# Cached key and value pages moved to other steps of a hybrid decoder layer

## The chip, the core and the metric

The kernel runs on one core of a Trainium2 chip. The metric is device time in microseconds of one execution; lower is better. The core's engines are TensorE (PE; PEld is its weight load), VectorE (DVE), ScalarE (ACT), GpSimd (POOL) and SyncE (SP); each runs its own instruction stream in order, and they wait for each other through semaphores. SyncE, ScalarE and GpSimd also issue DMAs, each into a queue of its own.

## The reference

One layer of a decoder for 512 new prompt rows and for eight sequences that add one row each to a past of 4096 rows. Cut to what matters:

```python
xn = rms_norm(x, norm1_g)
proj = xn @ w_in                                     # 2048 -> 5128 columns
u_pool, h_b, h_c, h_x, q, k, v, f_logit = split(proj)
y_pool = causal_pool_mix(u_pool, ...)                # window means, 4 groups
y_conv = h_b * causal_dwconv(h_c * h_x, ...)         # 3 taps
y_att = attn_fn(rms_norm(q), rms_norm(k), v, log_sigmoid(f_logit + b_f))
x = x + concat(rms_norm(y_pool), rms_norm(y_conv), rms_norm(y_att)) @ w_o
a, gate = split(rms_norm(x) @ w_up)
x = x + (silu(causal_dwconv(a, ...) + b) * gate) @ w_down
```

For the prompt, `attn_fn` is causal attention with 8 heads of 128 over the 512 rows themselves. For the eight sequences it is

```python
k_past = cache_k[l, page_table].reshape(db, past, N_HEADS, HEAD_DIM)
v_past = cache_v[l, page_table].reshape(db, past, N_HEADS, HEAD_DIM)
s = q . k - (decay of the forget gates);  p = softmax(s);  o = p @ v
```

with pages of 128 rows: 32 pages a sequence, 256 in all. A page of keys and a page of values is 512 KB each, so the caches are 268 MB of what the kernel reads.

## The kernel before

Prompt rows and sample rows stand side by side as 520 columns. Weights are loaded 2 MB at a time (`load_raw`, by SyncE), split into a head and a rest by ScalarE and VectorE (`head`, `weight_rest`), and multiplied on TensorE in three passes (`products`, `out_chunk`).

All engines walk through the same **steps** `s`, numbered 0 to 174, and at each step issue what belongs to it:

- steps 0 to 79: the input projection, a chunk of weights each;
- steps 82 to 93 (`MIX0` = 81, `HEAD0` = 93): the pooling and convolution mixers. `pool_part` runs on VectorE in steps 81, 84, 87 and 90, and TensorE's `pool_mix` one step later;
- steps 93 to 141: the eight prompt heads, one each six steps (`HSTEP`), seven stages each. Stage 1 is the sum of squares on TensorE, stage 4 the row maximum on VectorE, stage 5 the transposes, stage 6 the product with the values;
- step 142 (`TAIL`): the end of the mixers' norm; here SyncE also reloads the residual;
- steps 143 to 174 (`OUT0` on): the output projection, 32 chunks of 24 matmuls (`out_chunk`).

The cached pages are woven into these steps. `page_slots` fixes which page belongs to which step; from its tables `KEYS` and `VALUES` every engine takes its part:

- a **key page** is loaded by SyncE (`page`, line 584) into one of four buffers (`kring`), as soon as VectorE has used the page that was in it; VectorE's `key_page` (line 1802) multiplies it with the query and sums, head by head. In a step VectorE takes the first key page ahead of `pool_part` and `conv_part`, the second at the end of the step;
- a **value page** is loaded by GpSimd (`value_loads`, line 505) into one of four buffers (`vring`) as soon as TensorE has used the page in it; TensorE's `value_page` multiplies it with the probabilities. In the steps of the projection the first two pages stand within the chunk (after its third or fifth block) and the others behind it; in the steps of the heads, the first two of four stand ahead of the head's own matmuls, otherwise all stand behind them;
- `value_places` assigns the buffers. A value page whose step lies between the end of all keys (`K_END[-1]`) and `TAIL` goes round eight buffers, the four of the keys included; those in key buffers are loaded by SyncE (line 645), and the first of each waits until all 256 key pages are used. Before, no step fulfils the condition;
- when the last key page of a sequence has been used, a softmax over its 4096 scores runs in small pieces over the next eight steps (`softmax`, `misc`), and its values can begin six steps later; when its values end, sixteen small matmuls (`t_quad` in the rows) bring its output into columns one step later.

Before, a step has two key pages, and none from 82 to 93; the keys end at step 141. Value pages of the heads' steps come two at a time in two steps of three, and in all steps from 82 to 93 and from 142 on in the pattern 4, 4, 2; they end at step 169. Two lines of SyncE's loop load the first weights of the output projection in steps 107 and 111, beside the heads; six further loads of 2 MB follow in the projection (line 570), each after `sample_out`, a small product that stands behind every fourth chunk (the rows with `t_wraw` on TensorE).

Of the kernel before, what the change touches and what calls it, by code (L numbers as in the profile page):

```python
# [28 lines left out]
PAGES = PAST // P  # L29
# [20 lines left out]
CHUNKS = 80  # L50
MIX0 = CHUNKS + 1
HEAD0 = MIX0 + 12
STAGES = 7
HSTEP = 6
TAIL = HEAD0 + (HEADS - 1) * HSTEP + STAGES
KEY0 = 2
K_RATE = 2


def page_slots():  # L60
    keys, values, k_end, v_end = {}, {}, [], []
    slots = [s for s in range(KEY0, TAIL) if not MIX0 < s <= HEAD0]
    for n in range(DEC * PAGES):
        keys.setdefault(slots[n // K_RATE], []).append(n)
    for r in range(DEC):
        k_end.append(slots[(PAGES * (r + 1) - 1) // K_RATE])
    at = 0
    for r in range(DEC):
        at = max(at, k_end[r] + 6)
        done = 0  # L70
        while done < PAGES:
            rate = ((2 if at % 2 == 0 else 0) if at < CHUNKS else (2 if at % 3 else 0) if HEAD0 < at < k_end[-1] else
                    (4 if at % 3 else 2))
            take = min(rate, PAGES - done)
            if take:
                values[at] = [r * PAGES + done + i for i in range(take)]
            done += take
            at += 1
        v_end.append(at - 1)
    return keys, values, k_end, v_end  # L80


KEYS, VALUES, K_END, V_END = page_slots()
EARLY = TAIL - STAGES
OUT0 = TAIL + 1
# [2123 lines left out]
```

How the kernel before makes its waits and increments, by code:

```python
        def step(eng, count, ins):  # L340
            count.inc(ins)
            eng.wait_ge(count.sem, count.value())
# [81 lines left out]
        def copy_piece(eng, copy, q, n, j, done):  # L425
            eng.wait_ge(z_full, n + 1)
            bank = ps[:, 4 + n % 4, :]
            if j < 4:
                copy(orow[:, q, j, :], bank).then_inc(done, 1)
            else:
                copy(srow[:, q * 512:(q + 1) * 512], bank[0:DEC]).then_inc(done, 1)
# [4 lines left out]
        @block.gpsimd  # L436
        def _(pool):
            cst = Count(const_ready)
            cst.inc(pool.memset(ident[:, :], 0.0))
            cst.inc(pool.memset(ones[:, :], 1.0))
            cst.inc(pool.memset(cmask[:, :], 0.0))
            cst.inc(pool.memset(tri[:, :], 1.0))
            for t in range(16):
                cst.inc(pool.memset(rc[:, t:t + 1], 1.0 / (t + 1)))
            cst.inc(pool.memset(epsc[:, :], EPS))
            pool.wait_ge(const_ready, cst.value())
            cst.inc(pool.affine_select(out=ident[:, :], in_=ident[:, :], compare_op=ALU.not_equal, fill=1.0,
                                       base=0, pattern=[[-1, P]], channel_multiplier=1))
# [3 lines left out]
            cst.inc(pool.affine_select(out=tri[:, :], in_=tri[:, :], compare_op=ALU.is_ge, fill=0.0,  # L453
                                       base=0, pattern=[[-1, P]], channel_multiplier=1))
            pool.wait_ge(const_ready, cst.value())
            tv = tri.rearrange("p (a c) -> p a c", c=PAGES)
# [59 lines left out]
            pool.wait_ge(z_act, 3)
            for b in range(DEC):
```

## Time and profile before

| | us |
|---|---|
| median of 3 runs | 2842.98 |
| lowest and highest | 2842.80, 2843.91 |
| the profiled execution | 2841.29 |
| its span, first to last instruction | 2839.4 |
| TensorE busy | 2651.8 (93%) |
| VectorE busy | 1426.1 (50%) |
| ScalarE busy | 732.9 (26%) |
| DMA, mean rate over the span | 188 GB/s |

The mean shares hide the stages: the feed-forward from about 1300 us on is nearly all TensorE, and the traffic of the caches lies before it. So the table of the whole says little on this change; the rows further down are cut by stage. A busy share there is that of one stretch.

### The profile page before, as it was taken

Reading aid. Unit: us, or ns where it says so; the run is one execution under the profiler, and the core shown is the slowest. Engines: PE = TensorE matmul, PEld = TensorE weight load, DVE = VectorE, ACT = ScalarE, POOL = GpSimd, SP = SyncE. Lnnn points to the kernel's source line nnn. Section 1 sums busy time; section 2 is a strip of 40 time slices with the busy share of each in tenths; the row PEclk is TensorE's granted clock in tenths of the full one; section 3 lists DMA queues with packets and bytes.
Section 4 is the critical chain, followed back from the end, with each engine's and each line's share of the span. In section 5 each row is a group of like instructions: output and inputs, shape, how many; then the busy total and the mean of one; then the engine's idle time right before and its main releaser. Section 6 shows DMA issues by size and latency. Waiting matters only on the chain.

```text
span 2839.4 us, 50530 instructions
## 1 busy us (share of the span) xinstructions
PE 2651.8 (93%) x19656; PEld 2325.7 (82%) x19656; DVE 1426.1 (50%) x5629; ACT 732.9 (26%) x981; POOL 156.6 (6%) x317
## 2 busy tenths in 40 slices
PE   5899999977768699989999999999999999999998
PEld 3799989952333255659999999999999999999998
DVE  4787776765778732234434343434343434343433
ACT  4332212212333521133222222222222222222221
POOL 0100000012101122200000000000000000000000
PEclk7999999988867699989999999999999999999999
DMA  7689999998999887753222222222223222222221
GB/s 242 239 285 328 332 344 341 338 363 283 376 358 355 289 294 262 271 186 130 91 90 90 90 90 90 90 90 90 93 101 100 95 90 90 90 90 90 90 90 64
DMA packets 274531, 532.93 MB, mean 188 GB/s; under 512 B 16410, under 2 KB 177787, under 8 KB 272980
## 3 DMA queue, kind: packets, MB, share of 16 engines
q1 hardware_dynamic: 214573, 361.52, 37.1%
q0 software_dynamic: 39472, 142.46, 13.7%
q10 hardware_dynamic: 20247, 25.73, 2.5%
q8 instruction: 154, 2.52, 0.4%
q14 instruction: 85, 0.70, 0.1%
HBM read 503.94 MB, written 24.05 MB: 186 GB/s over the span
## 4 chain that ended last, share of the span: by engine, by line
PE 79%; DMA 7%; DVE 7%; issue 2%; ACT 2%; SPq 1%; ACTq 0%; POOL 0%; POOLq 0%; DVEq 0%
PE ps L711 78%; DVE t_work L1802 4%; DMA t_r<-in_cache_k 4%; DMA t_r<-in_cache_v 2%; DMA t_wraw<-in_w_in 1%; PE ps L714 1%; DVE t_xl L1639 0%; DVE t_stg L1695 0%; DVE t_nmax L1940 0%; SPq L584 0%; DVE t_wl L1639 0%; DVE t_work L1639 0%; DVE t_auxL L1947 0%; SPq L570 0%; ACT L1425 0%
## 5 line engine op out<-in xcount | busy, mean ns | idle before, releaser
L711 PE MATMUL ps<-t_xh,t_wh 128*128 128x260 f32 (+1 forms) x4352 | 949.1, 293 | 11.9 <-DVE t_xl L1639 11.8
L711 PE MATMUL ps<-t_xh,t_wl 128*128 128x260 f32 (+1 forms) x4352 | 935.7, 291 | 0.0
L711 PE MATMUL ps<-t_xl,t_wh 128*128 128x260 f32 (+1 forms) x4352 | 934.1, 290 | 0.0
L1639 DVE TENSOR_TENSOR t_wl<-t_wraw,t_wh 128x1024 fp32r<-128x1024 f32 x376 | 459.9, 1224 | 870.2 <-ACT t_wh L1236 870.2
L1236 ACT ACTIVATE t_wh<-t_wraw 128x1024 fp32r<-128x1024 f32 x376 | 398.1, 1060 | 1644.0 <-PE ps L711 1643.8
L711 PEld LDWEIGHTS ps<-t_xh,t_wh 128*128 128x128 f32 x4352 | 685.5, 190 | 94.2 <-issue 63.8
L711 PEld LDWEIGHTS ps<-t_xh,t_wl 128*128 128x128 f32 x4352 | 685.8, 189 | 11.8
L711 PEld LDWEIGHTS ps<-t_xl,t_wh 128*128 128x128 f32 x4352 | 685.4, 189 | 9.1
L1802 DVE CUSTOM_DVE_ANT_0 t_work<-t_r,t_work 128x128 f32<-128x128 f32 x2048 | 454.5, 285 | 154.9 <-DMA t_r<-in_cache_k 142.7
L711 PE MATMUL ps<-t_hh,t_wh 128*128 128x260 f32 x1408 | 285.8, 284 | 3.4 <-issue 3.4
L711 PE MATMUL ps<-t_hh,t_wl 128*128 128x260 f32 x1408 | 284.7, 284 | 0.0
L711 PE MATMUL ps<-t_hl,t_wh 128*128 128x260 f32 x1408 | 283.0, 282 | 0.0
L711 PE MATMUL ps<-t_r,t_work 128*8 128x512 f32 x1040 | 186.9, 670 | 67.2 <-DMA t_r<-in_cache_v 52.2
L1639 DVE TENSOR_TENSOR t_r<-ps,t_r 128x520 f32<-128x520 f32 (+1 forms) x184 | 128.5, 698 | 228.2 <-PE ps L711 228.2
L711 PEld LDWEIGHTS ps<-t_hh,t_wh 128*128 128x128 f32 x1408 | 218.3, 189 | 4.2 <-issue 3.7
L711 PEld LDWEIGHTS ps<-t_hl,t_wh 128*128 128x128 f32 x1408 | 217.3, 189 | 0.0
L711 PEld LDWEIGHTS ps<-t_hh,t_wl 128*128 128x128 f32 x1408 | 216.8, 189 | 0.0
L505 POOL DMA_DIRECT2D t_r<-in_cache_v x256 | 136.1, 532 | 959.2 <-PE ps L711 915.2
L1802 DVE DVE_READ_ACCUMULATOR2_ANT t_S<- 128x1 f32 x2048 | 164.6, 80 | 0.1
L711 PEld LDWEIGHTS ps<-t_r,t_work 128*8 128x8 f32 x1040 | 19.4, 88 | 148.7 <-DMA t_r<-in_cache_v 98.7
L520 POOL DMA_DIRECT2D out_ffn_sample<-t_aux x8 | 4.1, 518 | 1554.6 <-ACT t_aux L1236 1554.6
L1643 DVE SCALAR_TENSOR_TENSOR t_work<-t_work 128x8 f32<-128x8 f32 (+1 forms) x176 | 78.2, 486 | 3.1
(256 smaller groups left out, 1197.0 us busy)
## 6 DMA issues: line engine op xcount, KB each, us to landing
t_r<-in_cache_k SPq DMA_DIRECT2D x256, 512.0 KB, 7.2
t_r<-in_cache_v POOLq DMA_DIRECT2D x256, 512.0 KB, 6.5
t_wraw<-in_w_up SPq DMA_DIRECT2D x44, 2048.0 KB, 8.0
t_wraw<-in_w_in SPq DMA_DIRECT2D x22, 2048.0 KB, 11.6
t_wraw<-in_w_down SPq DMA_DIRECT2D x22, 2048.0 KB, 7.8
t_wraw<-in_w_o SPq DMA_DIRECT2D x11, 2048.0 KB, 12.2
scr_proj<-t_stg ACTq DMA_DIRECT2D x40, 256.0 KB, 5.5
t_aux<-scr_proj ACTq DMA_DIRECT2D x8, 768.0 KB, 18.4
```

The costliest lines, as they stand in the source:

```text
L505: pool.dma_start(vring[:, b, :], v_pages[bass.ds(g, 1), :, :].rearrange("a p n -> (a p) n")).then_inc(v_loaded[b], 16)
L520: pool.dma_start(o["ffn_sample"][0, b, 1, :].rearrange("(t n) -> t n", n=P), astrows[:, b, :]).then_inc(states_copied, 16)
L711: return pe.matmul(out, lhsT, rhs, start=start, stop=stop)
L714: return pe.transpose(out, in_, ident[0:n, 0:n])
L1236: return act.activation(out, in_, ACT.Copy)
L1639: return dve.tensor_tensor(out, in0, in1, op)
L1643: return dve.scalar_tensor_tensor(out, in0, scalar, in1, ALU.mult, ALU.add)
L1802: last = dve.tensor_tensor_reduce(out=junk[:, h * HD:(h + 1) * HD], in0=kring[:, p % RING, h * HD:(h + 1) * HD], in1=qcur[r % 2][:, h * HD ...
```

## The change

`page_slots` alone is changed. Its new table of slots gives a step one key page in steps 82 to 93 and two elsewhere (`K_RATE`), where there were none and two. With twelve more pages placed there, the keys end at step 135 instead of 141. Value pages keep their rule up to step 79 and, in fact, their places up to step 93; in the heads' steps while keys run they come two at a time in every odd step; from step 136 to 141 in the pattern 4, 4, 2, in eight buffers; from step 142 on four in every step, so that they end at step 165 instead of 169. In numbers: steps 94 to 135 hold 42 value pages (56 before), steps 136 to 141 hold 20 (10 before), step 142 holds 4 in both, and the projection 92 (88 before).

```diff
-    slots = [s for s in range(KEY0, TAIL) if not MIX0 < s <= HEAD0]
+    slots = [s for s in range(KEY0, TAIL) for _ in range(1 if MIX0 < s <= HEAD0 else K_RATE)]
     for n in range(DEC * PAGES):
-        keys.setdefault(slots[n // K_RATE], []).append(n)
+        keys.setdefault(slots[n], []).append(n)
     for r in range(DEC):
-        k_end.append(slots[(PAGES * (r + 1) - 1) // K_RATE])
+        k_end.append(slots[PAGES * (r + 1) - 1])
...
-            rate = ((2 if at % 2 == 0 else 0) if at < CHUNKS else (2 if at % 3 else 0) if HEAD0 < at < k_end[-1] else
-                    (4 if at % 3 else 2))
+            rate = ((2 if at % 2 == 0 else 0) if at < CHUNKS else (2 if at % 2 else 0) if HEAD0 < at < k_end[-1] else
+                    2 if at % 3 == 0 and at < TAIL else 4)
```

On TensorE, around steps 135 to 137, the order before was this (a row with `t_r,t_work` is a value page's product, two rows a page; `t_aux,t_ones 128x512 x2` are the sums of the last head's stage 1, `t_work,t_ones 128x512` is the total of a mixer's norm):

```order
L711 MATMUL ps<-t_auxL,t_aux 128x128
L714 MATMUL ps<-t_ident,t_aux 128x128 x4
L711 MATMUL ps<-t_work,t_ones 128x512
L711 MATMUL ps<-t_aux,t_ones 128x512 x2
L711 MATMUL ps<-t_r,t_work 8x512 x4
L711 MATMUL ps<-t_aux,t_ones 128x128
```

and it is this after the change:

```order
L711 MATMUL ps<-t_auxL,t_aux 128x128
L714 MATMUL ps<-t_ident,t_aux 128x128 x4
L711 MATMUL ps<-t_work,t_ones 128x512
L711 MATMUL ps<-t_r,t_work 8x512 x8
L711 MATMUL ps<-t_aux,t_ones 128x512 x2
L711 MATMUL ps<-t_r,t_work 8x512 x8
L711 MATMUL ps<-t_aux,t_ones 128x128
```

Four pages (138 to 141, eight rows) now stand ahead of the head's stage 1, the last two of them in key buffers.

On TensorE, at the seam between the heads and the projection, the piece before was this (`t_auxL,t_aux` are the last head's products with the values, `t_xh,t_wh` the projection's first matmul):

```order
L711 MATMUL ps<-t_quad,t_work 128x1 x8
L711 MATMUL ps<-t_auxL,t_aux 128x512
L711 MATMUL ps<-t_auxL,t_aux 128x384
L711 MATMUL ps<-t_auxL,t_aux 128x256
L711 MATMUL ps<-t_auxL,t_aux 128x128
L711 MATMUL ps<-t_r,t_work 8x512 x8
L711 MATMUL ps<-t_work,t_ones 128x512
L711 MATMUL ps<-t_r,t_work 8x512 x4
L711 MATMUL ps<-t_xh,t_wh 128x512
```

and it is this after the change:

```order
L711 MATMUL ps<-t_auxL,t_aux 128x512
L711 MATMUL ps<-t_auxL,t_aux 128x384
L711 MATMUL ps<-t_auxL,t_aux 128x256
L711 MATMUL ps<-t_auxL,t_aux 128x128
L711 MATMUL ps<-t_r,t_work 8x512 x8
L711 MATMUL ps<-t_work,t_ones 128x512
L711 MATMUL ps<-t_r,t_work 8x512 x4
L711 MATMUL ps<-t_ps,t_ones 128x8
L711 MATMUL ps<-t_quad,t_work 128x1 x8
L711 MATMUL ps<-t_xh,t_wh 128x512
```

The small matmuls of the sequence whose values end (`t_quad`), and a sum of the last softmax (`t_ps`), moved from ahead of the head's last stage to right ahead of the projection.

## Rows read from the trace of the kernel before

**Rows 1.** The page, 40 equal slices of 71 us, busy tenths.

```profile
PE   5899999977768699989999999999999999999998
DMA  7689999998999887753222222222223222222221
```

**Rows 2.** Windows by stage: length, then busy us (instructions) by engine, clock, DMA share, GB/s.

```profile
606.90:650.00 43.10, 26.85 (x110) 9.43 (x103) 21.46 (x84) 9.18 (x15) 8.07 (x16) 0.63 0.84 311
650.00:697.10 47.10, 33.04 (x144) 8.01 (x144) 21.75 (x53) 10.55 (x19) 17.39 (x33) 0.96 0.89 302
697.10:938.30 241.20, 180.83 (x631) 82.47 (x631) 190.19 (x1451) 82.66 (x155) 29.83 (x56) 0.75 0.98 364
759.00:806.00 47.00, 26.72 (x92) 11.86 (x91) 29.16 (x222) 14.04 (x26) 4.23 (x8) 0.71 1.03 389
938.30:981.00 42.70, 28.25 (x110) 14.00 (x112) 36.95 (x225) 23.33 (x38) 4.24 (x8) 0.68 0.69 231
1003.50:1239.20 235.70, 227.39 (x1196) 139.84 (x1194) 59.01 (x81) 43.05 (x58) 44.53 (x85) 0.99 0.74 257
```

**Rows 3.** Waits of TensorE in the mixers, 606.9 to 697.1: us, times, longest.

```profile
PE ps L711 <- DMA t_r<-in_cache_v: 25.1, 22, 5.4
PE ps L711 <- DVE t_auxW L1889: 1.9, 1, 1.9
```

**Rows 4.** Waits of VectorE, 697.1 to 938.3; the last row, 755 to 808.

```profile
DVE t_work L1802 <- DMA t_r<-in_cache_k: 32.4, 20, 7.0
DVE t_work L1639 <- ACT t_stg L1404: 5.1, 3, 4.2
DVE t_aux L1934 <- ACT t_aux L1429: 3.3, 1, 3.3
DVE t_denall L1827 <- PE ps L711: 2.5, 1, 2.5
...
DVE t_work L1802 <- DMA t_r<-in_cache_k: 21.4, 8, 7.0
```

**Rows 5.** The page, costliest groups: all key pages on VectorE, eight instructions a page.

```profile
L1802 DVE CUSTOM_DVE_ANT_0 t_work<-t_r,t_work 128x128 f32<-128x128 f32 x2048 | 454.5, 285 | 154.9 <-DMA t_r<-in_cache_k 142.7
```

**Rows 6.** Projection: TensorE's waits, then its timeline at a late and a timely pair.

```profile
PE ps L711 <- DMA t_r<-in_cache_v: 2.4, 3, 1.2
...
1050.77 0.40 PE L711 MATMUL ps<-t_xh,t_wl 128*128 128x512 f32 x1
1051.73 1.03 PE L711 MATMUL ps<-t_r,t_work 128*8 128x512 f32 x4 [0.56 <-DMA t_r<-in_cache_v]
...
1054.93 0.50 PE L711 MATMUL ps<-t_xh,t_wh 128*128 128x512 f32 x1
...
1199.15 0.40 PE L711 MATMUL ps<-t_xh,t_wl 128*128 128x512 f32 x1
...
1200.45 0.50 PE L711 MATMUL ps<-t_xh,t_wh 128*128 128x512 f32 x1
```

**Rows 7.** Timeline: end of VectorE's last key instruction of step 135, then TensorE to the projection.

```profile
937.80 0.08 DVE L1802 DVE_READ_ACCUMULATOR2_ANT t_S<- 128x1 f32 x1
...
937.88 1.99 PE L711 MATMUL ps<-t_aux,t_ones 128*128 128x512 f32 x4 [0.33 <-ACT t_aux L1421]
...
967.06 1.90 PE L711 MATMUL ps<-t_r,t_work 128*8 128x512 f32 x8 [9.04 <-issue]
...
972.59 3.41 PE L711 MATMUL ps<-t_quad,t_work 128*128 128x1 f32 x16
...
989.33 1.88 PE L711 MATMUL ps<-t_r,t_work 128*8 128x512 f32 x4 [2.71 <-DMA t_r<-in_cache_v]
```

**Rows 8.** SyncE's weight loads from 1010; issues at 1039 to 1041 and 1044 to 1046, landing us.

```profile
1010.38 171.02 SPq L570 DMA_DIRECT2D t_wraw<-in_w_o  x6
...
t_r<-in_cache_v POOLq DMA_DIRECT2D x2, 512.0 KB, 4.4
...
t_r<-in_cache_v POOLq DMA_DIRECT2D x2, 512.0 KB, 7.9
```

## Prediction

> **What bounds the kernel now.** I read the page's 40 slices first, to find the place: TensorE is at 9 tenths in nearly every slice, but at 6 to 9 tenths in slices 8 to 13, while the DMA row stands at 8 or 9 until slice 16 and at 2 to 3 after that [rows 1]. The change lies wholly in slices 8 to 17; the feed-forward behind them isn't touched. Then I cut that part by stage [rows 2]: the mixers (steps 82 to 93, 90.2 us in two halves), the heads while keys still run (steps 94 to 135, 241.2 us), the last head (steps 136 to 141, 42.7 us), the seam before the output projection, and the projection (235.7 us). Each has a limit of its own.
>
> - **Mixers**: no engine is full. TensorE waits 25.1 us for value pages [rows 3]. The four value buffers are reloaded as fast as pages land; the DMA share is 0.84 and 0.89 [rows 2].
> - **Heads with keys**: DMA share 0.98 at 364 GB/s, and VectorE busy 190.2 of 241.2 us [rows 2]. So both are near full. VectorE waits 32.4 us for key pages, of which 21.4 us fall into the 53 us in which two weight loads of the output projection pass [rows 4].
> - **Last head**: DMA is idle for a third of the time (0.69) and VectorE is busy for 37.0 of 42.7 us [rows 2].
> - **Projection**: TensorE is busy 227.4 of 235.7 us [rows 2], with DMA waits of 2.4 us in all [rows 6]. Here a page costs what its matmuls cost.
>
> **The change, part by part.** The sum is made against the profiled run, 2841.3 us with its span of 2839.4 us; it lies 1.7 us below the median of 2842.98.
>
> *Mixers, twelve key pages more: +10 us.* A page is 512 KB. While DMA was full, 47.0 us at 389 GB/s [rows 2], a page took 0.524 MB / 389 GB/s = 1.35 us, so twelve are 16.2 us of DMA time. Before, four keys (pages 160 to 163) were loaded ahead here and left lying; now each used key frees a buffer and starts another load. Two or so of those loads fall into the first half, where 16% of 43.1 us is idle and hides them. Ten fall into the second: 13.5 us, and idle there is 11% of 47.1 us, 5.2 us. The remaining 8.3 us lengthen the landings of the value pages, on which TensorE already waits. On VectorE a key page is 454.5 us / 256 = 1.8 us [rows 5]; VectorE is idle for more than half of the stretch, so eleven of the twelve are hidden, but the one in step 84 stands ahead of the second pooling part, for which TensorE waited 1.9 us [rows 3]: +1.9. Bounds: 0, if DMA takes all twelve in its gaps, and 16.2 + 1.9 = 18.1, if none. I take 10, since the nearest row, the second half, says that the gaps there are small.
>
> By the Trainium skill ("DMA: Bandwidth & Descriptors", Specifications), a core draws about 358 GB/s from its memory at most. By that the mixers have (358 - 306) GB/s x 90.2 us = 4.7 MB to spare for 6.3 MB, and the rest would take 4.4 us, so this term would be 6 and not 10 (306 being the mean of the two halves). The trace moved 389 GB/s for 47 us [rows 2], so that is no ceiling here, and the measurement decides.
>
> *Heads with keys, 42 value pages for 56: -15 us.* Values come every second step instead of two steps in three: 14 pages fewer, and at the end no four keys are loaded ahead: 18 x 1.35 = 24.3 us of DMA time out of 241. Two keys a step stay, so VectorE's work stays. The gain is in its waits. Outside the weight loads these are 32.4 - 21.4 = 11.0 us in short pieces, and a tenth less traffic should leave 2: -9. Beside the weight loads three pages are gone: 3 x 1.35 = -4. TensorE has two pages fewer for each head, mostly hidden: -2. Then VectorE is next: 190.2 us busy, some 12 us in the small gaps between instructions, and about 11 us of waits for ScalarE and TensorE [rows 4] make 213, so more than -28 can't be. Bounds: -8 and -28.
>
> *Last head and seam: +4 us.* All keys are used at the end of step 135, and six steps hold 20 value pages instead of 10. Eight buffers serve them, four being the keys' own; but pages 140 to 143 come first, in exactly those four, and TensorE must use 140 and 141 at the head of step 136, ahead of the head's own matmuls. Before, VectorE ended the keys of step 135 at 937.9 us, and TensorE began the sums of the last head at 937.88 [rows 7]. Now the first load can be issued only then; a pair lands in a median of 4.4 us when DMA is light [rows 8], at 942.6 and 943.8 or so with the issue. TensorE brings 2 us of its own (two pages are new in step 135), waits some 3 us, and uses two more pages: the sums start near 944.4, +6.5 us. Behind that, ten more pages are 8 to 10 us of TensorE (0.95 us each: two pages are eight matmuls in 1.90 us), but TensorE stood idle for 9.04 us before 967.06 [rows 7], and they go there. Keys no longer delay VectorE; still ScalarE's normalizations stand in the same chain, so I give 2.5 us back, no more. In the seam TensorE waited 2.71 us before 989.33 for a page that was late [rows 7]; that wait goes, and the sixteen small matmuls of an ended sequence, which before stood in step 140 (at 972.59, 3.41 us [rows 7]), now stand right ahead of the projection: 0. Bounds: -5 (the idle 9 us vanish and the first loads land early), +9 (nothing is given back).
>
> *Projection, four pages in every step: +14 us.* 46 pairs of pages instead of 44 stand in it. A pair holds up the projection's matmuls by 1.3 us (1199.15 to 1200.45 [rows 6]): +2.6. The larger part is late pages. Each four steps SyncE issues a 2 MB weight load, six in this stretch [rows 8], right before the second pair of a step is used and reloaded. The loads issued next to it took 7.9 us, against 4.4 us without [rows 8]. With four pages in two successive steps the same buffers are due one step later, and that is too soon: from 1050.77 to 1054.93 is 4.2 us instead of 1.3, 2.9 us lost [rows 6]. Before, the pattern 4-4-2 met this fully once in six, the other times a step with two pages or other work lay between. Now all six meet it: 6 x 2.9 = 17.2, less about 5 us paid before, less a little for what the stall itself lets land: +11. Bounds: +2.6 (the loads land in time) and +15.
>
> Sum: 10 - 15 + 4 + 14 = +13, so 2854 us for a profiled run and 2855.5 us for the median.
>
> **The rivals.**
> - *DMA time is only moved (faster).* Keys hide in the mixers' gaps, and the page landings nowhere grow. For it: 12 us of DMA time are idle there; VectorE's waits show that the heads want it. The price: mixers +2, heads -20, last head +4, projection +2.6: -11, 2832 us. It decides if value pages in the mixers still land about as fast with keys beside them. Against it: TensorE already waits on just these landings.
> - *Key waits vanish almost entirely (no change).* Heads -26 instead of -15, the rest as forecast: +2, 2845 us. For it: 24.3 us of DMA time freed. Against: two thirds of the waits belong to two 2 MB loads, which stay.
> - *The last head pays in full (slower still).* Mixers 15, heads -10, last head 9, projection 14: +28, 2871 us.
> - *The change doesn't do what it says*: the order of the instructions shows keys ending at step 135 and the pages moved as told, so I give this no chance of its own.
>
> **How the numbers follow.** Forecast (2849 to 2863 us): 0.48. Faster rival, everything below 2837.3: 0.17. No change, 2837.3 to 2848.7: 0.21. Slower still, above 2863: 0.14. About 0.2% is what a measurement of this kernel can tell from no change. So faster 0.17, same 0.21, slower 0.62. The range from 2834 to 2869 leaves out a tenth on each side: below it lies the faster rival with the heads at their bound, above it the last one with all ends together.
>
> **What would show it.** In the changed kernel's profile: the mixers, from the last projection tile to the first head, near 100 us, with a DMA share near 1.0 and key pages used by VectorE between the pooling parts; if it stays at 90, the first term is wrong. The heads to the end of the keys near 226 us, VectorE's waits for keys under 20 us; if these are still 30 the second is wrong. A wait of TensorE of about 3 us for a value page just ahead of the last head's sums. In the projection waits for value pages of 10 us or more, in about six pieces, once every four steps, each just after a weight load was issued. If the pages land within 6 us there, the forecast is too slow by 11 us.

## The result, and the profile after

The changed kernel takes 2863.49 us (median of 6 runs, 2858.39 to 2876.21) against 2841.03 us for the kernel before (6 runs, 2836.38 to 2843.91, the three of the table before among them). The ratio is 1.0084 with a 95% interval of 1.0061 to 1.0107: slower by 22.5 us by the medians, where the sum had +13. The time lies 8 us above the forecast of 2855.5 us and inside the range of 2834 to 2869. It is half a microsecond above 2863, where the rival "slower still" was to begin, so the direction was right and something in the sum was too hopeful.

The profiled execution is the slowest of the six, 2876.2 us with a span of 2874.5 us. Its two rows of slices (tenths busy, 40 slices, here 72 us each) answer to [rows 1]: TensorE still dips in slices 9 to 14, and the DMA row has an 8 for a 9 in slices 11 and 13, within the heads.

```profile
PE   5899999976767699998999999999999999999998
...
DMA  6789999998898787735222223222222232222221
```

By stage (same columns as [rows 2]; mixers, heads with keys, last head and seam, projection to the end of the attention's last product for the sample rows, which in the kernel before ends at 1263.2):

```profile
608.80:714.20 105.40, 65.38 (x248) 19.81 (x245) 63.69 (x330) 19.72 (x34) 24.69 (x47) 0.70 0.90 332
714.20:951.50 237.30, 173.95 (x566) 87.04 (x565) 190.44 (x1451) 81.73 (x154) 21.13 (x40) 0.69 0.89 325
951.50:1010.20 58.70, 41.13 (x183) 15.09 (x182) 20.78 (x44) 34.03 (x51) 7.39 (x14) 0.80 0.72 262
1010.20:1298.30 288.10, 269.61 (x1380) 165.67 (x1379) 76.22 (x104) 56.10 (x75) 48.61 (x92) 0.96 0.68 239
```

The same stretches before were 90.2, 240.8, 55.4 and 269.9 us, and what lies behind them is 1576.2 us in both. So the profile shows +15.2, -3.4, +3.3, +18.2, and 1.9 us from ahead of the mixers. The heads are the surprise: DMA there fell from 0.98 to 0.89 and hardly any time came back.

The waits name the places. Mixers, TensorE (us in total, times, longest):

```profile
PE ps L711 <- DMA t_r<-in_cache_v: 33.5, 17, 6.0
PE ps L711 <- DVE t_auxW L1889: 3.6, 1, 3.6
```

Against 25.1 and 1.9 us [rows 3]. Heads with keys, VectorE, then TensorE:

```profile
DVE t_work L1802 <- DMA t_r<-in_cache_k: 16.0, 12, 6.2
DVE t_work L1639 <- ACT t_stg L1404: 12.1, 4, 3.7
DVE t_aux L1934 <- ACT t_aux L1429: 3.4, 1, 3.4
DVE t_nmax L1940 <- PE ps L711: 2.8, 1, 2.8
DVE t_ps L1844 <- ACT t_work L1577: 2.6, 1, 2.6
DVE t_maxall L1824 <- PE ps L711: 2.0, 1, 2.0
...
PE ps L714 <- DVE t_auxL L1947: 48.9, 7, 10.0
PE ps L711 <- ACT t_aux L1426: 9.4, 7, 1.6
```

VectorE's waits for keys halved (32.4 before [rows 4]), but its waits for ScalarE and TensorE grew to 23 us. TensorE no longer waits for value pages at all. In the kernel before it did, and the last line of its table was smaller by 30.6 us:

```profile
PE ps L711 <- DMA t_r<-in_cache_v: 21.7, 11, 4.7
PE ps L714 <- DVE t_auxL L1947: 18.3, 6, 11.8
```

The transposes of a head (L714) wait for VectorE to scale the probabilities (L1947), once a head. What TensorE was spared in page waits, and more, it now spends there: the wait was replaced, not removed.

At the head of step 136 the forecast wait stands, ahead of the sums of the last head (timeline: start, length, and in brackets the wait ahead):

```profile
951.94 1.04 PE L711 MATMUL ps<-t_r,t_work 128*8 128x512 f32 x8
955.58 1.03 PE L711 MATMUL ps<-t_r,t_work 128*8 128x512 f32 x4 [2.59 <-DMA t_r<-in_cache_v]
959.22 1.88 PE L711 MATMUL ps<-t_r,t_work 128*8 128x512 f32 x4 [2.62 <-DMA t_r<-in_cache_v]
961.03 3.48 PE L711 MATMUL ps<-t_aux,t_ones 128*128 128x512 f32 x4
```

And in the projection TensorE waits, in total and at one of six late pairs, behind a timely one for comparison (the weight load was issued at 1066.22):

```profile
PE ps L711 <- DMA t_r<-in_cache_v: 12.7, 14, 1.9
PE ps L711 <- DVE t_work L1639: 5.8, 1, 5.8
...
1068.86 0.40 PE L711 MATMUL ps<-t_xh,t_wl 128*128 128x512 f32 x1
1069.19 1.04 PE L711 MATMUL ps<-t_r,t_work 128*8 128x512 f32 x8
1070.16 0.50 PE L711 MATMUL ps<-t_xh,t_wh 128*128 128x512 f32 x1
...
1073.52 0.40 PE L711 MATMUL ps<-t_xh,t_wl 128*128 128x512 f32 x1
1074.74 1.03 PE L711 MATMUL ps<-t_r,t_work 128*8 128x512 f32 x4 [0.82 <-DMA t_r<-in_cache_v]
1076.45 1.03 PE L711 MATMUL ps<-t_r,t_work 128*8 128x512 f32 x4 [0.67 <-DMA t_r<-in_cache_v]
1077.41 0.50 PE L711 MATMUL ps<-t_xh,t_wh 128*128 128x512 f32 x1
```

The timely pair takes 1.30 us between the projection's matmuls, the late one 3.89. The brackets own up to 1.49 us of the 2.59 lost. The other 1.1 us is in no wait: a page that comes alone takes 1.03 us, as long as two that come together (1.04). In the trace's single records the matmuls of a timely pair start four and four, 0.43 us apart, and those of a single page two and two, at the same distance: two pages that are there together run side by side. This pair is one of the cheaper ones: read in the same way, the six lose 2.2 to 4.5 us, 19.7 in all.

### The profile page after: what moved, and what is told of

It reads as the page before. It is cut to its first block, busy times and chain, and to the rows that moved or that the text cites. A ratio compares the mean times of both kernels' runs of the same rounds, so it can differ in the third digit from the quotient of the medians.

```text
span 2874.5 us, 50529 instructions
## 1 busy us (share of the span) xinstructions
PE 2666.9 (93%) x19656; PEld 2337.7 (81%) x19656; DVE 1425.3 (50%) x5629; ACT 733.2 (26%) x981; POOL 149.4 (5%) x305
## 3 DMA queue, kind: packets, MB, share of 16 engines
q0 software_dynamic: 37744, 136.17, 12.8%
## 4 chain that ended last, share of the span: by engine, by line
PE 71%; DMA 12%; DVE 10%; issue 3%; ACT 2%; SPq 1%; ACTq 0%; POOL 0%; POOLq 0%; DVEq 0%
PE ps L711 70%; DMA t_r<-in_cache_k 7%; DVE t_work L1802 6%; DMA t_r<-in_cache_v 4%; DMA t_wraw<-in_w_in 1%; PE ps L714 1%; DVE t_wl L1639 1%; DVE t_xl L1639 0%; DVE t_stg L1695 0%; SPq L580 0%; DVE t_nmax L1940 0%; SPq L570 0%; DVE t_S L1802 0%; DVE t_work L1639 0%; ACT t_wh L1236 0%
## 5 line engine op out<-in xcount | busy, mean ns | idle before, releaser
L711 PE MATMUL ps<-t_xh,t_wh 128*128 128x260 f32 (+1 forms) x4352 | 951.1, 294 | 12.5 <-DVE t_xl L1639 12.4
L711 PE MATMUL ps<-t_r,t_work 128*8 128x512 f32 x1040 | 179.5, 665 | 55.5 <-DMA t_r<-in_cache_v 52.0
L505 POOL DMA_DIRECT2D t_r<-in_cache_v x244 | 129.0, 529 | 981.1 <-PE ps L711 942.4
```

The source lines that it names most:

```text
L505: pool.dma_start(vring[:, b, :], v_pages[bass.ds(g, 1), :, :].rearrange("a p n -> (a p) n")).then_inc(v_loaded[b], 16)
L711: return pe.matmul(out, lhsT, rhs, start=start, stop=stop)
```

## The experiments

The kernel before was run beside each group; its median there was 2839.2, 2844.6 and 2843.4 us, so times are compared as ratios to it.

| kernel | median, us | ratio, 95% interval | mixers | heads | last head, seam | projection |
|---|---|---|---|---|---|---|
| before | 2841.0 | 1 | 90.2 | 240.8 | 55.4 | 269.9 |
| after | 2863.5 | 1.0084, 1.0061 to 1.0107 | 105.4 | 237.4 | 58.7 | 288.1 |
| after_again | 2865.5 | 1.0090, 1.0065 to 1.0115 | 101.5 | 235.9 | 56.4 | 283.4 |
| proj_442 | 2858.2 | 1.0060, 1.0039 to 1.0080 | 106.5 | 234.0 | 59.2 | 277.4 |
| before_proj4 | 2849.1 | 1.0036, 1.0021 to 1.0050 | 89.4 | 240.8 | 58.1 | 277.5 |
| thin_keys | one run, 2854.9 | | 95.4 | 230.6 | 56.8 | 280.8 |
| heads_even | 2864.7 | 1.0068, 1.0046 to 1.0090 | 99.7 | 233.3 | 59.2 | 278.5 |
| keys_only | 2863.5 | 1.0055, 1.0037 to 1.0073 | 103.2 | 235.6 | 73.2 | 265.7 |
| rings_swapped | 2867.4 | 1.0067, 1.0048 to 1.0087 | 101.5 | 233.3 | 62.5 | 284.3 |
| keys_late | 2861.4 | 1.0067, 1.0047 to 1.0086 | 104.8 | 231.7 | 59.4 | 283.6 |
| before_sq | 2836.2 | 0.9981, 0.9967 to 0.9995 | 87.1 | 241.8 | 54.1 | 262.2 |
| before_avoid | 2834.5 | 0.9978, 0.9964 to 0.9992 | 89.0 | 241.6 | 53.8 | 264.6 |
| before_avoid_sq | 2833.4 | 0.9955, 0.9935 to 0.9975 | 89.6 | 238.6 | 58.2 | 255.3 |
| proj_avoid_sq | 2845.6 | 1.0011, 0.9999 to 1.0024 | 102.4 | 231.8 | 58.5 | 261.5 |

The stages are us of one profiled execution each. Equal stages of different kernels repeat within 7 us, the same heads from 231.7 to 237.4, so a stage is judged by the mean of the kernels that share it, and a stage that only one kernel has can be told no better than that.

### The changed kernel again

No edit. 

> The changed kernel once more, unaltered, for a profile nearer its median and to see how its time repeats. Both theories below share this run as their base. Expected: 2858 to 2866 us, 1.0065 to 1.010 of the kernel before; mixers 103 to 106 us, heads with keys 233 to 238, last head and seam 57 to 60, projection to the last attention product 282 to 288.

2865.5 us, as expected; mixers and last head lie 1.5 and 0.6 us below their ranges. Its mixers are 4 us and its projection 5 us shorter than in the first profile: +11.3, -4.9, +1.0 and +13.5 against the kernel before, where the first profile has +15.2, -3.4, +3.3 and +18.2.

### Late pages in the projection: proj_442 and before_proj4

proj_442 is the changed kernel with

```diff
-                    2 if at % 3 == 0 and at < TAIL else 4)
+                    2 if at % 3 == 0 and at < 160 else 4)
```

> The changed kernel, but with the value pages of the projection in the pattern 4, 4, 2 up to step 159 and four a step only behind it. Theory (late pages behind weight loads): four of the six places where two steps with four pages follow a weight load are gone, so the waits for value pages in the projection fall from 12.7 to some 5 us and the time by 8 to 14 us against the changed kernel (to about 2850). Rival (the projection's growth is only the pages moved there, or a clock that falls whatever the pattern): within 4 us of the changed kernel.

before_proj4 is the kernel before with the new pattern in the projection alone:

```diff
-                    (4 if at % 3 else 2))
+                    2 if at % 3 == 0 and at < TAIL else 4)
```

> The kernel before, with one part of the change alone: four value pages in every step of the projection. The same number of pages stands there as before (88), so there is no price for pages moved. Theory (late pages behind weight loads): +10 to +16 us against the kernel before, with waits for value pages of 10 us or more in the projection, one group of 1.5 to 3 us behind each weight load. Rival (only the number of pages counts): within 3 us of the kernel before.

proj_442: the projection is 277.4 us, 7.5 under the mean of four kernels with the change's projection (284.9; thin_keys, with the same projection, had 280.8), and the ratio falls from 1.009 to 1.006. That is a little less than expected, as were the waits: 8.1 us remain, not 5. The intervals of the two ratios overlap, so this run alone doesn't decide. before_proj4: +10 us (6 to 14 by the interval), its projection +7.6, with the same number of pages in it. So the pattern costs, without a page brought in from another stage. Its waits, a little under the 10 us expected, and one of its five late pairs fit the mechanism:

```profile
PE ps L711 <- DMA t_r<-in_cache_v: 8.4, 10, 1.4
...
1060.31 1.03 PE L711 MATMUL ps<-t_r,t_work 128*8 128x512 f32 x4 [0.67 <-DMA t_r<-in_cache_v]
1062.01 1.03 PE L711 MATMUL ps<-t_r,t_work 128*8 128x512 f32 x4 [0.67 <-DMA t_r<-in_cache_v]
```

The rival, that only the number of pages counts, falls.

### What DMA is worth in mixers and heads: thin_keys

Key pages 164 to 255 are loaded to an eighth; scores made of the rest are old data.

```diff
-                sp.dma_start(ring[:, p % RING, :],
-                             pages[bass.ds(g, 1), :, :].rearrange("a p n -> (a p) n")).then_inc(loads[p % RING], 16)
+                w = 1024 if r * PAGES + p < 164 else 128
+                sp.dma_start(ring[:, p % RING, 0:w],
+                             pages[bass.ds(g, 1), :, 0:w].rearrange("a p n -> (a p) n")).then_inc(loads[p % RING], 16)
```

> The changed kernel, in which the loads of key pages 164 to 255 carry an eighth of their columns (so the scores of those pages are made from old data). All instructions and waits stay, 92 x 459 KB of traffic are taken away from the mixers and heads. Theory for the mixers (the twelve key pages cost DMA time): they fall from 105 to 92 us or less; rival (the cost is VectorE's order ahead of the pooling part, 1.9 us a step): they stay above 100. Theory for the heads (the chain through ScalarE, VectorE and TensorE is the limit once DMA is relieved): 237 falls to 220 to 230 and no further, VectorE's waits for keys to under 4 us. Rival (DMA still sets the heads): they fall below 215.

```profile
613.00:708.50 95.50, 61.78 (x252) 17.48 (x249) 63.78 (x330) 19.84 (x34) 25.44 (x48) 0.78 0.84 298
708.50:939.10 230.60, 169.92 (x561) 85.15 (x560) 190.55 (x1451) 81.06 (x152) 21.14 (x40) 0.70 0.54 179
...
DVE t_work L1640 <- ACT t_stg L1405: 17.4, 5, 4.5
DVE t_ps L1845 <- ACT t_work L1578: 5.1, 2, 2.9
...
DVE t_work L1803 <- DMA t_r<-in_cache_k: 1.9, 2, 1.3
```

(The lines are one further down than in the other kernels.) In the heads the DMA share falls to 0.54 and the key waits to 1.9 us, and still the stretch takes 230.6 us: VectorE's waits for ScalarE alone grew to 24 us. So relief of the key loads cannot bring it much below 231 in this order of work, as far as one profile tells; what then sets the length is the work that the engines do for each other, as the theory had it; the rival's 215 falls. In the mixers 7.5 us of 13.8 (by the means further down) go with the bytes, not all: neither theory holds whole. TensorE's time in this stage is its busy time and its waits: 59.9 and 30.1 us in the kernel before, 65.4 and 39.9 in the changed one, 61.8 and 33.7 here, at a mean granted clock of 0.80, 0.70 and 0.78. So a third of what the mixers lost in the first profile is no wait at all: the same matmuls took longer, with a lower clock on the mean and with pages that come singly; how much each did is not separated.

### Which part of the change helps the heads: keys_only

The new key slots with the value rule of before:

```diff
-            rate = ((2 if at % 2 == 0 else 0) if at < CHUNKS else (2 if at % 2 else 0) if HEAD0 < at < k_end[-1] else
-                    2 if at % 3 == 0 and at < TAIL else 4)
+            rate = ((2 if at % 2 == 0 else 0) if at < CHUNKS else (2 if at % 3 else 0) if HEAD0 < at < k_end[-1] else
+                    2 if at % 3 == 0 else 4)
```

> The keys of the change, one a step beside the mixers, with the value pages by the rule of before (two steps of three in the heads, 4, 4, 2 from there on). Pages then stand so: 56 in the heads with keys, 20 in the last head, 76 in the projection (88 before). Theory (the keys beside the mixers cost 11 to 15 us and buy little in the heads): mixers 101 to 106 us, heads with keys 236 to 241, last head and seam 57 to 60, projection 262 to 265 (six pairs fewer, 1.3 us each); in all 3 to 12 us over the kernel before. Rival (thinning the values, not the keys, is what costs, by the order in odd steps): heads 228 or less, and the whole 3 us or more under the kernel before.

```profile
715.40:950.90 235.50, 176.00 (x630) 80.71 (x628) 190.39 (x1451) 81.86 (x154) 29.59 (x56) 0.76 0.98 365
...
971.39 1.90 PE L711 MATMUL ps<-t_r,t_work 128*8 128x512 f32 x8 [7.47 <-issue]
...
970.71 0.58 ACT L1236 ACTIVATE t_work<-ps 128x512 f32<-128x512 f32 x1
```

The steps of the heads hold 58 value pages here, not the 56 that I expected. They take as long with these 58 and DMA at 0.98 as with 42 and DMA at 0.9. Thinning the values bought next to nothing. What the heads did gain fits the bytes: 364 GB/s x 240.8 us = 87.7 MB before, 365 x 235.5 = 86.0 here. The difference of 1.7 MB, about three pages, takes 4.6 us at that rate, and 5.2 were gained: 80 key loads are issued in the stretch and 83 before (the four loaded ahead at the end before, for step 136, have no successor now). The next 8.9 MB, down to the 77.1 MB of the changed kernel (325 x 237.3), bought 1.5 us, as its heads took 234.0 us on the mean of six kernels. Both differences are small against the scatter of equal heads; that sixteen pages fewer bought no more than three is what can be told.

Mixers, heads and projection came within a microsecond of what was expected, and the rival falls. But the whole is 16 us over the kernel before, not 3 to 12, because the last head took 73.2 us, 15 more than the mean of the changed kernel's. The first page of a sequence must wait until ScalarE has copied out the output of the sequence before (the third row: 970.71 + 0.58 = 971.29, TensorE goes on at 971.39), and that copy stands behind a head's work on ScalarE. This wait is half of the 15 us; the other half stays open. Here the boundary of two sequences falls into step 137; in the changed kernel it falls into step 142 and waits 3.39 us. The 9.04 us before 967.06 in [rows 7] were that same wait, with ScalarE's copy ending at 966.96.

### The order in the heads: heads_even

```diff
-            rate = ((2 if at % 2 == 0 else 0) if at < CHUNKS else (2 if at % 2 else 0) if HEAD0 < at < k_end[-1] else
+            rate = ((2 if at % 2 == 0 else 0) if at < CHUNKS else (0 if at % 2 else 2) if HEAD0 < at < k_end[-1] else
```

> The changed kernel with the pairs of value pages in steps 94 to 135 in the even steps instead of the odd ones, so that none stands between a head's stage 0 and the sums of its stage 1. Same number of pages, same keys, same traffic. Theory (the heads are a chain TensorE sums, ScalarE, VectorE, and pages in the odd steps delay the sums): VectorE's waits for ScalarE's square of a mixer's rows (11.5 us in the changed kernel, 5.1 before) fall to about 5, the heads with keys from 236 to 226 to 231 us, and the time by 5 to 10 us against the changed kernel. Rival (VectorE's own work with its key waits is the limit, whatever the parity): heads within 3 us of 236.

```profile
707.40:940.70 233.30, 165.30 (x569) 87.00 (x568) 190.32 (x1451) 80.94 (x152) 21.22 (x40) 0.71 0.92 332
...
DVE t_work L1802 <- DMA t_r<-in_cache_k: 28.5, 15, 6.9
DVE t_work L1639 <- ACT t_stg L1404: 3.4, 3, 1.7
```

The wait for ScalarE fell to 3.4 us, as the theory has it, but the wait for keys rose by 12.5 us, and the heads stayed at 233.3. (The even steps hold 44 value pages, not the same 42: the number moved by two with the parity.) VectorE's waits behave here as one pool of slack: where one of them shrinks, another fills it. Neither side was right about both wait and time; the length was the rival's.

### The last head: rings_swapped

```diff
-        b = n % (2 * RING if K_END[-1] < slot_of[n] < TAIL else RING)
+        b = (n + RING) % (2 * RING) if K_END[-1] < slot_of[n] < TAIL else n % RING
```

> The changed kernel with other buffers for the pages of steps 136 to 141: pages 140 to 143 go to value buffers, and 144 to 147, a step later, to the key buffers. Theory (TensorE waits at the head of step 136 for pages that could be issued only when VectorE had used the last keys): the waits of 2.0 and 1.4 us ahead of the last head's sums go, and last head with seam falls from 57 to 59 us to 53 to 56; the time by 2 to 5 us, about what can be told. Rival (the last head is bound by ScalarE's and VectorE's chain; the wait is only moved behind the sums): last head with seam within 1 us of the changed kernel.

```profile
946.14 1.98 PE L711 MATMUL ps<-t_aux,t_ones 128*128 128x512 f32 x4
954.30 1.88 PE L711 MATMUL ps<-t_r,t_work 128*8 128x512 f32 x4 [6.18 <-DMA t_r<-in_cache_v]
```

The sums start without a wait, and the page behind them then waits 6.18 us, ahead of the head's next matmuls. The stage is 62.5 us, 4 above the mean of the changed kernel, so neither side had it. The key buffers come free only with the last key, and whoever uses them first pays.

### The rest of the mixers: keys_late

```diff
-                if kp:
+                if kp and not MIX0 < s <= HEAD0:
                     key_page(*kp[0])
...
-                for n in kp[1:]:
+                for n in kp[0 if MIX0 < s <= HEAD0 else 1:]:
                     key_page(*n)
```

> The changed kernel, in which VectorE takes the key page of a step beside the mixers at the end of the step, behind the pooling and convolution parts and not ahead of them. Traffic is the same. Over six kernels with the mixers of the change these took 99.7 to 106.5 us, mean 103, against 90 without the keys and 95.4 with seven eighths of the key bytes left out. Theory (that rest of 5 us is VectorE's order: two more key pages' time ahead of pooling parts on which TensorE waits): TensorE's wait for the pooling part falls from 3.6 to about 2 us or goes, mixers 97 to 101. Rival (the rest is the clock and small loads still queued; DMA is all of it): mixers 101 to 106, and a wait for value pages of 28 to 35 us as before.

```profile
PE ps L711 <- DMA t_r<-in_cache_v: 36.4, 19, 6.1
...
PE ps L711 <- DVE t_auxW L1889: 1.9, 1, 1.9
```

The pooling wait is back at 1.9 us, and the mixers took 104.8: the page waits took up what it released. VectorE's order is not what the mixers pay for, or not where DMA is full. Of the price that thin_keys kept, 5.3 us against the profile before, 3.6 are waits of TensorE (3.1 of them for value pages) and 1.9 longer matmuls; why pages still came later there, with an eighth of the key bytes, stays open.

### The two edits in the projection

"sq" moves TensorE's sum of squares of the sample rows (`LAST + 2`), for which it waits 5.8 us in both kernels, a step later. "avoid" puts two pages into the step behind a weight load and four into the others:

```diff
-                if s == LAST + 2:
+                if s == LAST + 3:
                     pe.wait_ge(y_norm, YA_SQ)
...
-                    (4 if at % 3 else 2))
+                    2 if (at % 3 == 0 if at < TAIL else at > TAIL and (at - TAIL) % 4 == 3) else 4)
```

> The kernel before with two edits in the projection alone: two value pages in the one step of four that follows a weight load and four in the others (the last page then stands in step 167, not 169), and TensorE's product for the sum of squares of the sample rows one step later, behind VectorE's work for it. Theory (late pages behind weight loads, and a wait of 5.8 us for VectorE that stands in both kernels): no wait for a value page over 1 us, the wait for VectorE gone, and 4 to 9 us under the kernel before. Rival (clock and page count set the projection, the waits are filled by other stalls): within 3 us of the kernel before.

> The kernel before, with one edit alone: TensorE's product for the sum of squares of the sample rows one step later. In the kernel before it waits 5.8 us for VectorE there, and the matmuls after it run 7 times at 0.43 us and not 0.23. Theory (wait and slow matmuls both go): 5.8 + 1.4 = 7 us, 2830 to 2838 against a kernel before of 2838 to 2845. Rival (the wait comes back a step later, or the end of the output projection waits for something else): within 3 us of the kernel before.

> The kernel before, with the other edit alone: two value pages in the step that follows a weight load and four in the others. The waits for value pages were 2.4 us in the projection of the kernel before, and the one late pair cost 2.9 us. Theory (late pages are the only thing in the pattern that costs): waits under 1 us and 2 to 6 us under the kernel before. Rival (the gain of both edits together, 13 us, came from the product moved): within 2 us of the kernel before.

> The changed kernel with both edits in the projection: two value pages in the one step of four behind a weight load, four otherwise, and the product for the sum of squares one step later. Theory (six late pairs of 2 to 2.9 us behind weight loads, and the wait of 5.8 us with slow matmuls behind it): projection from 278 to 288 down to 262 to 266 us, no wait for a value page over 1 us in it, and 15 to 22 us under the changed kernel, so 0 to 8 us over the kernel before, by what the mixers cost and the heads don't give back. Rival (the growth of the projection lies in page count and clock): 7 us under the changed kernel, by the product moved alone.

The windows of the projection in before_avoid_sq and in proj_avoid_sq:

```profile
997.20:1252.50 255.30, 254.69 (x1369) 161.48 (x1367) 75.33 (x103) 55.58 (x75) 47.03 (x89) 1.00 0.76 262
...
1004.70:1266.30 261.60, 258.55 (x1380) 160.87 (x1379) 76.26 (x104) 56.17 (x75) 48.84 (x92) 1.00 0.75 263
```

sq alone gives -5 us by its ratio (-1 to -9 by the interval, -7.7 in the stage), where 7 were expected; the trace shows its wait gone. avoid alone gives -6 (-2 to -10, and -5.3 in the stage), at the edge of the 2 to 6 expected, and the waits for value pages fall from 2.4 to 0.2 us; together -13 (-14.6 in the stage), about their sum and more than the 4 to 9 I had given them. With both, TensorE waits for value pages 0.2 us in the whole projection. Applied to the changed kernel they bring its projection from 284.9 to 261.5 us and its ratio from 1.0084 to 1.0011. By the ratios that is 21 us, within the 15 to 22 expected, and the rival's 7 falls. Of the 23.4 us in the stage, 7.7 belong to sq, if it is worth here what it is worth in the kernel before, and 15.7 to late pages. What is then left over before_avoid_sq are the mixers (+12.8), the projection (+6.2, with two pairs of pages more in it and 1.8 us of page waits) and, against them, the heads (-6.8). before_avoid_sq beats both kernels: 0.9955 (0.9935 to 0.9975), some 13 us.

## Why the prediction was right, and where it was wrong

By the means over the kernels that share a stage (five or more for the stages ahead of the projection; for the projection four after, without thin_keys, and a single profile before):

| term | forecast | bounds given | mean before and after | measured |
|---|---|---|---|---|
| mixers | +10 | 0 to 18.1 | 89.1, 102.9 | +13.8 |
| heads with keys | -15 | -8 to -28 | 240.7, 234.0 | -6.7 |
| last head and seam | +4 | -5 to +9 | 55.9, 58.4 | +2.5 |
| projection | +14 | +2.6 to +15 | 269.9, 284.9 | +15.0 |
| sum | +13 | | | +24.6 |

The sum of the stages agrees with the medians (+22.5, by the interval 17 to 30 us). Of the 12 us by which the sum was short, 8 are in the heads, whose term lies outside its own bounds; the other three lie inside theirs or at the edge.

- **Mixers: right in place, near in size.** The wait for value pages grew from 25.1 to between 31 and 36 us, the DMA share to about 0.9, the length to 103 us (forecast: near 100). By thin_keys some 7 us of it are the bytes (one profile, and equal mixers differ by as much), and a third of the first profile's loss is longer matmuls, which the sum didn't have. The 1.9 us for VectorE's order were not a term of their own: with keys_late that wait goes and the time doesn't. The term came 4 us higher, and the gaps that I meant to fill stayed: the DMA share was 0.84 to 0.89 before and 0.88 to 0.93 after, with TensorE waiting for pages in both. So a share of 0.9 left no room here. Why it stays below 1.0 no run shows.
- **Heads: the term that failed.** The step that was wrong is that freed DMA time comes back as time. I counted freed DMA time as if it returned until VectorE was full, and set the floor at 213 us by taking the 11 us of waits for ScalarE and TensorE in [rows 4] as a constant. The key waits fell as forecast (under 20 us), and so did the bytes, by 10.6 MB or 20 pages in the first profile; but the 11 us were no constant: they grew to 23 in the changed kernel, and in thin_keys to 30 of 32 us of waits. The floor is about 231, not 213. The waits for other engines that [rows 4] show beside the longer wait for keys were only the part which that wait didn't already cover. What was won, some 5 us, came with the three key loads fewer at the end; the thinned value pages bought about 1.5.
- **Last head and seam: right in size, in part by luck.** The wait for the key buffers was forecast at some 3 us and took 5.2 and 3.4 us in the two profiles of the changed kernel; pages did fill idle time. Only the idle 9.04 us weren't free: it was the wait of a sequence's first page for ScalarE's copy, and it went away because the boundary moved to step 142, where 3.39 of it came back. In keys_only, with the boundary in step 137, this stage took 15 us more; the forecast didn't look at where a boundary falls.
- **Projection: right, with its mechanism.** Six late pairs behind six weight loads, 2.2 to 4.5 us lost at each (2.9 assumed), 19.7 in all, against some 4.6 at two late pairs before; 11.4 of the 12.7 us of waits stand there. before_proj4 has the cost without the added pages, and avoid takes it away: 15.7 us in the changed kernel less 5.3 in the kernel before is 10.4, against 11 forecast.

Of the rivals, the faster one had the mixers wrong, and "no change" needed -26 us in heads whose floor allows -10. "Slower still" had the better numbers for mixers (15) and heads (-10), but its reason, a last head that pays in full, didn't come: the last head paid 2.5 us.

The Trainium skill's figure of about 358 GB/s for a core ("DMA: Bandwidth & Descriptors", Specifications, where it is half of what a stack gives to two cores) would have made the mixers' term 6; they paid 13.8, at 323 to 347 GB/s. In the heads of keys_only the trace has 365 GB/s over 235.5 us, and before_avoid_sq 368 over 238.6, a little above the figure, over far longer than the 47 us at 389 GB/s: with this one core running it was no ceiling.

## What to carry to other kernels

Before crediting freed transfer time to a stage, ask what the stage takes when the transfer costs nothing, and don't take the floor from the other waits in the same table: they grow as the first one shrinks. Thinning the loads to an eighth is a cheap run that measures this floor. Look also at what the engine's own work costs when it waits more: part of the price here was longer matmuls, not waits. Where a ring of buffers is refilled beside a periodic large load, put the lighter step right behind that load; a late buffer costs more than its named wait.

## What the runs showed of the hardware

A wait cost TensorE more than its length here. In the kernel before, sq's wait of 5.76 us is followed by seven matmuls that start 0.43 us apart, where those behind them start 0.23 to 0.24 apart; the granted clock from 1239 to 1241.95 is 0.50, the lower of its two levels (1.2 GHz), and from 1244 to 1250 it is 1.00, the upper (2.4 GHz):

```profile
1239.23 0.69 PE L711 MATMUL ps<-t_work,t_ones 128*128 128x64 f32 x2 [5.76 <-DVE t_work L1639]
...
1241.53 0.63 PE L711 MATMUL ps<-t_xl,t_wh 128*128 128x512 f32 x1
1241.95 0.63 PE L711 MATMUL ps<-t_xh,t_wl 128*128 128x512 f32 x1
...
1244.02 0.40 PE L711 MATMUL ps<-t_xh,t_wh 128*128 128x512 f32 x1
1244.26 0.39 PE L711 MATMUL ps<-t_xl,t_wh 128*128 128x512 f32 x1
...
1239.00:1241.95 2.95, 2.72 (x7) 2.25 (x8) 0.31 (x2) 0.00 (x0) 0.00 (x0) 0.50 0.00 0
```

At 0.20 us each that is 1.4 us on top of 5.8, and the stage was 7.7 us shorter without it. In before_avoid_sq, with no such wait left, the mean granted clock of the projection was 1.00, against 0.96 in the changed kernel. I had counted waits alone.

Shorter waits can do the same. After those at the late pair shown above (0.82 and 0.67 us) the matmuls start 0.23 us apart as before: there the loss is the pages that come singly, not the clock. But at two of the six late pairs of the same profile, behind first waits of 1.62 and 1.91 us, the clock fell as well. At the second of them the next page's product takes 1.88 us in place of 1.03, and nine matmuls of the projection behind it start 0.42 to 0.60 us apart:

```profile
1113.11 1.03 PE L711 MATMUL ps<-t_r,t_work 128*8 128x512 f32 x4 [1.91 <-DMA t_r<-in_cache_v]
1114.81 1.88 PE L711 MATMUL ps<-t_r,t_work 128*8 128x512 f32 x4 [0.67 <-DMA t_r<-in_cache_v]
...
1114.80:1120.20 5.40, 5.39 (x12) 2.92 (x13) 0.00 (x0) 0.00 (x0) 1.05 (x2) 0.50 0.83 273
```

A wait of 1.51 us, behind one of 0.70, at another pair (1151.29 to 1154.79) left the matmuls 0.23 us apart; what decides between the two stays open.
